# Low parts of streamed weights, computed in joined VectorE instructions in the wide stages of a decoder layer

## What is computed

```python
mixed = sigmoid(g_attn) * (attn @ w_attn_o) + sigmoid(g_ssm) * (ssm @ w_ssm_o)
h = h + rms_norm(mixed @ w_out)
f = rms_norm(h)
h = h + rms_norm((silu(f @ w_gate) * (f @ w_up)) @ w_down)
gate = sigmoid(rms_norm(h) @ w_ple_gate)
h = h + rms_norm((p @ w_ple) * gate)
```

## Time and profile before

| | |
|---|---|
| median of 3 runs | 1994.02 us (1993.68 to 1994.37) |
| profiled execution, first to last instruction | 1992.0 us |
| ScalarE busy | 1147.6 us, 58% |
| data moved | 394.74 MB, mean 198 GB/s |
| granted TensorE clock | 0.999, the upper level (2.4 GHz) throughout |

### The profile page before, as it was taken

One profiled execution on the slowest core, in us unless ns is written; L12 is line 12 of the kernel. 1 busy time (PEld: TensorE's weight loads), 2 busy tenths in 40 slices (PEclk: granted clock), 3 DMA queues, 4 the chain that ended last, 5 costly groups with the idle time before them and its releaser, 6 DMA issues.

```text
span 1992.0 us, 29428 instructions
## 1 busy us (share of the span) xinstructions
PE 1979.0 (99%) x10149; PEld 1681.0 (84%) x10149; DVE 1668.8 (84%) x2336; ACT 1147.6 (58%) x1482; POOL 18.9 (1%) x37
## 2 busy tenths in 40 slices
PE   9999999999999999999999999999999999999998
PEld 8888888888888888998888888888888888888886
DVE  7788888889888868767777787999999988888887
ACT  6666566666655545565545565556555555555575
POOL 0000000000000000000000000000000000000000
PEclk9999999999999999999999999999999999999999
DMA  8666676666566566545556667666566666766754
GB/s 235 200 191 190 190 206 184 188 192 195 172 207 209 189 203 223 156 132 156 191 191 239 205 207 242 189 202 202 190 201 200 200 201 201 254 201 207 244 189 152
DMA packets 255197, 394.74 MB, mean 198 GB/s; under 512 B 28840, under 2 KB 161440, under 8 KB 252928
## 3 DMA queue, kind: packets, MB, share of 16 engines
q1 hardware_dynamic: 251104, 369.87, 59.7%
q0 software_dynamic: 3824, 23.43, 3.5%
q10 hardware_dynamic: 176, 0.20, 0.0%
HBM read 387.08 MB, written 6.36 MB: 198 GB/s over the span
## 4 chain that ended last, share of the span: by engine, by line
PE 98%; DVE 1%; ACT 0%; DMA 0%; issue 0%; DVEq 0%; SPq 0%; ACTq 0%
PE acc L655 16%; PE acc L851 15%; PE acc L853 15%; PE acc L852 15%; PE acc L660 8%; PE acc L912 6%; PE acc L913 6%; PE acc L914 6%; PE acc L1107 1%; PE acc L785 1%; PE acc L637 1%; PE acc L636 1%; PE acc L638 1%; PE acc L1038 1%; PE acc L1242 0%; PE acc L714 0%
## 5 line engine op out<-in xcount | busy, mean ns | idle before, releaser
L1914 DVE TENSOR_TENSOR wlo<-raw,whi 128x1024 fp32r<-128x1024 f32 (+2 forms) x559 | 662.5, 1205 | 110.8 <-ACT whi L1351 108.3
L1351 ACT ACTIVATE whi<-raw 128x1024 fp32r<-128x1024 f32 (+1 forms) x560 | 572.2, 1044 | 244.4 <-PE acc L853 81.7
L655 PE MATMUL acc<-u,whi 128*128 128x512 f32 x1376 | 328.7, 391 | 0.0
L851 PE MATMUL acc<-whi,u 128*128 128x512 f32 x824 | 323.0, 392 | 0.1
L853 PE MATMUL acc<-whi,u 128*128 128x512 f32 x824 | 320.8, 389 | 0.0
L852 PE MATMUL acc<-wlo,u 128*128 128x512 f32 x824 | 320.6, 389 | 0.0
L655 PEld LDWEIGHTS acc<-u,whi 128*128 128x128 f32 x1376 | 252.7, 188 | 48.8
L851 PE MATMUL acc<-whi,g 128*128 128x512 f32 x520 | 202.8, 390 | 0.1
L853 PE MATMUL acc<-whi,g 128*128 128x512 f32 x520 | 202.4, 389 | 0.0
L852 PE MATMUL acc<-wlo,g 128*128 128x512 f32 x520 | 202.3, 389 | 0.0
L1374 ACT ACTIVATE whi<-raw 128x1024 fp32r<-128x1024 f32 x72 | 76.5, 1062 | 209.9 <-PE acc L914 162.0
(11 more groups left out here) (597 smaller groups left out, 2990.8 us busy)
## 6 DMA issues: line engine op xcount, KB each, us to landing
raw<-w_in_in SPq DMA_DIRECT2D x208, 512.0 KB, 3.8
raw<-w_gate_in SPq DMA_DIRECT2D x176, 256.0 KB, 3.0
raw<-w_up_in SPq DMA_DIRECT2D x176, 256.0 KB, 3.3
raw<-w_down_in SPq DMA_DIRECT2D x88, 512.0 KB, 4.6
raw<-w_ssm_o_in SPq DMA_DIRECT2D x64, 512.0 KB, 4.3
raw<-w_in_in SPq DMA_DIRECT2D x64, 256.0 KB, 4.0
raw<-w_attn_o_in SPq DMA_DIRECT2D x32, 512.0 KB, 4.7
raw<-w_out_in SPq DMA_DIRECT2D x32, 512.0 KB, 4.9
```

The lines of the kernel that those rows point to most:

```text
L655: return T.matmul(bank(banks[i]), wh[:, j, i * P:i * P + P], src[:, kts[j], :, :].rearrange("p a s -> p (a s)"), start=start and j == 0, s ...
L851: T.matmul(o, x_hi, wh[:, j, :], start=start, stop=False, skip_group_check=True)
L1351: S.activation(whi[:, slot, 0:w], raw[:, slot, 0:w], ACT.Copy).then_inc(sem("hi_ready"), 1)
L1914: V.tensor_tensor(wlo[:, slot, 0:w], raw[:, slot, 0:w], whi[:, slot, 0:w].bitcast(F32), ALU.subtract) \
```

## The change

In phases `so`, `ao`, `ff` and `dn` the low part of a plain pair is made in one instruction of 2048 columns when the odd chunk's turn comes, after both high parts; the even chunk's turn does nothing. `wo` and `pg` keep one low part for each plain chunk. In all sevens the two low parts of raw blocks become one of 1536 columns, which now stands after the third and the fourth sum, and the two low parts of the sums become one of 2048. Each joined instruction counts its semaphore by two at once. Nothing changes on TensorE, ScalarE or SyncE.

```diff
+PAIRED = ("so", "ao", "ff", "dn")
...
+            three = slice(CHUNK * slot + 512, CHUNK * slot + 2 * CHUNK)
             V.tensor_tensor(t[:, 0:2, :], raw_f[:, inner].rearrange("p (a n) -> p a n", a=2),
                             raw[:, slot, 0:512].unsqueeze(1).to_broadcast([P, 2, 512]), ALU.add) \
                 .then_inc(sem("t_sum"), 1)
-            dve.wait_ge(sem("hi_ready"), num(phase, it, c) + 1)
-            V.tensor_tensor(wlo_f[:, inner], raw_f[:, inner], whi_f[:, inner].bitcast(F32), ALU.subtract) \
-                .then_inc(sem("lo_ready"), 1)
             dve.wait_ge(sem("t_sum"), 3 * n + 1)
             V.tensor_tensor(t[:, 2, :], t[:, 0, :], raw[:, slot + 1, 0:512], ALU.add).then_inc(sem("t_sum"), 1)
             dve.wait_ge(sem("t_sum"), 3 * n + 2)
             V.tensor_tensor(t[:, 3, :], t[:, 2, :], raw[:, slot + 1, 512:], ALU.add).then_inc(sem("t_sum"), 1)
             dve.wait_ge(sem("hi_ready"), num(phase, it, c + 1) + 1)
-            V.tensor_tensor(wlo[:, slot + 1, 512:], raw[:, slot + 1, 512:], whi[:, slot + 1, 512:].bitcast(F32),
-                            ALU.subtract).then_inc(sem("lo_ready"), 1)
+            V.tensor_tensor(wlo_f[:, three], raw_f[:, three], whi_f[:, three].bitcast(F32), ALU.subtract) \
+                .then_inc(sem("lo_ready"), 2)
             if between:
                 between()
-            for half in range(2):
-                dve.wait_ge(sem("t_hi"), 2 * n + 1 + half)
-                two = slice(2 * half, 2 * half + 2)
-                V.tensor_tensor(t_lo[:, two, :], t[:, two, :], t_hi[:, two, :].bitcast(F32), ALU.subtract) \
-                    .then_inc(sem("t_lo"), 1)
+            dve.wait_ge(sem("t_hi"), 2 * n + 2)
+            V.tensor_tensor(t_lo[:, :, :], t[:, :, :], t_hi[:, :, :].bitcast(F32), ALU.subtract) \
+                .then_inc(sem("t_lo"), 2)
...
+        def pair_low(phase, it, c):
+
+            slot = c % RING - 1
+            dve.wait_ge(sem("hi_ready"), num(phase, it, c) + 1)
+            V.tensor_tensor(wlo[:, slot:slot + 2, :], raw[:, slot:slot + 2, :], whi[:, slot:slot + 2, :].bitcast(F32),
+                            ALU.subtract).then_inc(sem("lo_ready"), 2)
+
         def wide_low(phase, it, c, between=None):
 
-            if not is_seven(phase, it, c):
+            if is_seven(phase, it, c):
+                if c % 2 == 0:
+                    seven_sums(phase, it, c, between)
+            elif phase not in PAIRED:
                 split(phase, it, c)
-            elif c % 2 == 0:
-                seven_sums(phase, it, c, between)
+            elif c % 2:
+                pair_low(phase, it, c)
```

## The result

The changed kernel takes 2046.8 us (median of 4 runs, 2045.3 to 2052.8) against 1993.9 for the one before: 1.027 times as long, 95% interval 1.0256 to 1.0285. The profiled execution's span is 2043.7 us, 51.7 more than before.

The account below looks back on a forecast made before the run. TensorE, busy 1979.0 of 1992.0 us, was taken as the bound. Stalls of 42 plus 6 for loads made 48, so 2040, and 2042 with the median 2.0 above the span; 80 in 100 from 2014 to 2062.

Parts of the forecast that it names:

- The gain is worth nothing: 278 joins give back 0.07 us of VectorE each, 19 us; worth 0, as TensorE wasn't waiting for these low parts.
- The operand 0.23 us ahead: Weights load during the matmul before, so an operand must be there 0.23 us ahead of its first matmul.
- Steady cycle, 0: Plain pair plus seven, 10.20 us: joined sums' low parts keep 0.4 us of cover, plain pair 0.9; no cost.
- ff, 27.0: Stalls in ff passes: chunk 2 10.8, first sevens 7.2 and 5.4, chunk 14 3.1, ff 10 chunk 12 0.5 us.
- so, 6.9: Stalls in so: first half chunk 8 2.3, chunk 12 0.5, chunk 18 2.0; second half chunk 2 2.1 us.
- ao, 3.8: Stalls in ao: first seven, behind the gate on ScalarE, 2.1 us; three smaller ones 1.7 us.
- dn, 4.6: Stalls in dn: chunk 2 0.8, chunk 10 0.9, chunk 40 twice 1.0, dn 0's first seven 0.9 us.
- Absorption, taken as none: All stalls: whole 42.3 us kept; the rival that they absorb one another gave 21 us, 2015, chance 0.12.
- The loads, 6 us: Sevens outside ff: both slots come free at once, so refills cost 0 to 13.5 us, taken as 6; ff loads 0.
- the ring: A seven's slot refill loop: issue 0.15, landing 5.5 to 6.1, start 0.1, sums and low parts 4.33: 10.1 to 10.7 us.
- rival 2: Loads overlap freely and the ring stays under 10.2 us: 42 us slower, 2036; chance 0.25.
- rival 1: Loads limit in full: sevens pay 0.5 us or more each, late landings once hidden are paid: 66, 2060; chance 0.2.

Follow-up runs that it names:

- sums-only kernel: Against the kernel before, only the low parts of the sevens' four sums joined; raw low parts and plain chunks as before: 2029.4 us, ratio 1.018.
- joined signals only: Kernel before with no instruction joined or moved; in plain pairs of so, ao, ff, dn the odd low part signals for both: 2022.4 us, ratio 1.0141.
- kernel with covered joins: Changed kernel with joins kept only where the first half had cover, 172 of 278, halves elsewhere: 2001.5 us, ratio 1.0039 to the kernel before.

## Why the prediction was right

The forecast was 2042 us (range 2014 to 2062) for a measured 2046.8. Its mechanism held at nearly every place it named. That the sum came as near as 48 to 51.7 is partly luck: places it missed and places it overrated offset each other, and its term for the loads had the wrong mechanism.

- **The gain is worth nothing.** VectorE's joins take the computed times (1.75 and 2.29 us), but its busy time fell by 7 us, not by 19 to 20. Added up, the shown durations fell by 37.5 us, but the busy time counts the overlap of neighbours once, and that overlap fell by 30.4 us: 403 neighbours no longer overlap, where I had counted the 278 that the joins take away. On TensorE it would have been worth nothing either way.
- **The operand 0.23 us ahead.** In the stalls the first matmul starts 0.06 us after the low part's end (1522.97 and 1523.03 above), and the one behind it follows after 0.34 us (1523.37) instead of 0.23. A late low part thus costs its lateness plus 0.17 us, for the 0.23 of the sum; the terms change little, for another reason than the one given.
- **Steady cycle, 0.** It stayed at 10.20 us where no load was late, and the cover computed for the sums' low part was enough. The sums-only kernel shows that this rested on the moved raw low parts.
- **ff, 27.0.** Measured 26.95. Chunks 0 to 3 in passes 2 to 10: 10.8 against 10.7. First sevens: 7.2 and 5.4 against 7.6 and 5.6. Chunk 14: 3.1 against 1.7, partly absorbed. ff 10 chunk 12: 0.5 against 0.45. A late load at ff 7 chunk 12, 0.8, wasn't in the sum. Passes 5 to 9 run 44.5 us without it, passes 2 to 4 45.9 to 46.2; "about 45" was right between them.
- **so, 6.9.** Measured 5.1. Chunk 8 was taken as 2.3 us and is 0.6 (chunk 4 adds 0.25). The low part 8 stood before the operand sums; without it they moved up and end at 573.0 instead of 574.5. High part 9 moved up too, to 573.0 from 574.3, because its load landed 7.3 us after its issue instead of 9.7, and the joined part starts at 573.1. I had kept the old start of both. Where the sums keep their place, as with joined signals only, the wait costs 2.6. Chunk 12 0.5 (0.5), chunk 18 1.5 (2.0), second half 2.0 (2.1).
- **ao, 3.8.** Measured 6.4. The first seven is 2.1, as computed, and the three smaller ones are 0.44, 0.69 and 0.44 for 0.5, 0.7 and 0.5. Missed were the second half's chunk 2, 0.9, and chunk 12, 1.9: there ScalarE rounds the operands of `wo` for 1.49 us between the even and the odd high part, which holds back only the odd chunk until the join ties the even one to it.
- **dn, 4.6.** Measured 10.9, of which 4.5 is chunk 38 (2.9 the late load, 1.6 the lower clock behind it). The other terms came out at 6.1: 1.2, 0.9, 0.9, 1.25 and 1.2 against 0.8, 0.9, 0.9, 1.0 and 1.0, and chunk 42 (0.6) new.
- **Absorption, taken as none.** Right for the ff terms named, because VectorE's late instruction there is released by TensorE. Plain pairs and sevens alone add up to 8.6 us more than together, so it exists, but between places I had mostly not counted.
- **The loads, 6 us.** The size was near, the mechanism wrong. I put the second landing 5.5 to 6.1 us after the first issue and took the ring as partly over 10.20. The loads of a seven in the steady stretch now go out 0.58 us apart:

```profile
L545 SPq DMA_DIRECT2D raw<-w_ssm_o_in x2: 333/333/333, 640.3 to 640.9; - x2
...
DMA to landing us min/median/max: 3.6/4.0/4.4
```

The second lands 4.4 us after its own issue, 5.0 after the first's. With 0.15, 0.1 and 4.33 us that is a ring of 9.6, under 10.20, and the first sums are released by TensorE (above). This isn't so everywhere: over the whole kernel a load comes last before the first sums in 18 of the 72 sevens, against 3 before, in one of them here in `so` (625.79), where the second landing took 5.2 us. My bound read the second landing off pairs 0.9 and 1.1 us apart as if the landing were fixed and the spacing free. So rival 2 was right on the pace of the steady cycle. What cost time instead is what rival 1 named in half a sentence: single late landings that more cover used to hide: one of 9.8 us at dn 1 chunk 38, which costs 2.9, and 0.5 to 1.0 each in `wo`, `wz`, ff 7 and `pg`, where VectorE or ScalarE wait for loads that took 5.4 to 9.5 us. That is 5.9 for the 6 of the sum, a match of size by luck. The 1.6 us of the lower clock had no term at all. The sum was 48 for a measured 51.7: 1.5 by which loads and clock together exceed the 6, `ao` 2.6, dn's other terms 1.5, less 1.8 in `so`.
- **Faster** (rival 5) and **no change** (rival 4) had nothing behind them; every place I had computed came out on its side, covered or uncovered, mostly within 0.4 us.

## What to carry to other kernels

Joining two instructions of a producer is worth its fixed cost (here 0.07 us each) only if the producer's engine is the bound; and it delays the first half by at least the length of the second. Ask at every place where the joined form would stand, above all at the starts of passes and behind work that another engine has put between the two inputs, how long the consumer had been able to wait; the steady cycle says nothing about them. Where a gap in cover is closed, look next at the slowest landing that the old cover hid, not at the median one. And look at the granted clock behind a long wait of TensorE before giving its whole loss to the wait: here it was 1.6 of 4.5 us.

## What the runs showed of the hardware

- The cost of a VectorE subtraction grows by the column with a small fixed part: 512 columns 0.68 us, 1024 1.22, 1536 1.75, 2048 2.29. The joined instruction has no further price on TensorE: replaced by two with one signal it gives the same time to 0.6 us.
- Two 512 KB weight loads 0.58 us apart land 3.6 and 4.4 us after their own issue in a quiet stretch (3.5 to 4.0 and 4.3 to 4.8 in the five pairs after it in `so`; up to 5.2 for the second in the pairs before it). Beside a 1 MB load from GpSimd's queue single weight loads took 7.0 to 9.8 us in four kernels, and behind three GpSimd loads at once (2.5 MB) 10.3 to 11.2. In the changed kernel's stretch from 540 to 1935 us, 12 weight loads took over 7 us, against 7 before; 10 of the 12 had a GpSimd transfer under way beside them, and so had all 7 of before. It isn't the only company that does it: in the kernel with covered joins two loads took 7.4 and 7.6 us with none beside them. What in the DMA system makes them wait (order in the queues, or shared bandwidth) these runs don't tell.
- Whether such a pair is hit depends on less than a microsecond: in two traces the same GpSimd load cost nothing when it was issued 0.7 us after the second weight load, and 4.2 us (2.5 through the wait, 1.6 through the clock) when issued 0.5 us before it. This lets small changes far from an edited line show up as losses of 1 to 4 us in `dn`.
- During or just behind some waits of TensorE, from 1.8 to 6.7 us long in these traces, its granted clock is at the lower level for a stretch, and 512-column matmuls start 0.43 us apart instead of 0.23. One such stretch costs 1.5 to 1.6 us when it is full of them (3.65 against 2.07 us at ao's first seven, 3.76 against 2.18 at ff 4's). The same wait of 1.8 us was followed by it in three kernels and not in four; what decides it these traces don't tell.
